# Expert routing: high and low part of the activations side by side in one 512-column product

## The reference

```python
s1, i1 = lax.top_k(s[:, :, 0], 16); s2, i2 = lax.top_k(s[:, :, 1], 16)
cand_s = (s1[..., :, None] + s2[..., None, :]).reshape(T, 8, 256)
top_s, pos = lax.top_k(cand_s, 16)
gate = softmax(top_s)
hid = einsum('td,thkd->thk', x, u[idx])
y = einsum('thk,thkd->td', gelu(hid) * gate, v[idx])
```

## Time and profile before

| | us |
|---|---|
| median of 3 runs (lowest, highest) | 2159.97 (2158.83, 2162.43) |
| the profiled execution, its own time | 2154.51 |
| its span, first to last instruction | 2152.7 |
| Gelu of tile 0 to Gelu of tile 127 in `peer_hidden` (start to start) | 1370.2 to 1785.58 |
| TensorE busy in the span | 1963.3 (91%) |
| VectorE busy in the span | 1616.8 (75%) |
| ScalarE busy | 982.0 (46%) |
| GpSimd busy | 437.4 (20%) |
| mean granted clock of TensorE, of full speed | 0.955 |

### The profile page before, as it was taken

The page is one execution under the profiler, slowest core; times in us unless marked ns, Lnnn a source line. Parts: engine busy times, 40 slices in busy tenths (PEclk is TensorE's granted clock), DMA queues, the critical chain, the costliest instruction groups (busy, mean ns, idle before and its releaser), DMA issues. The chain is left out here.

```text
span 2152.7 us, 40884 instructions
## 1 busy us (share of the span) xinstructions
PE 1963.3 (91%) x16381; PEld 1775.2 (82%) x16381; DVE 1616.8 (75%) x2682; ACT 982.0 (46%) x1758; POOL 437.4 (20%) x238
## 2 busy tenths in 40 slices
PE   8967899989779998998788888999999999999997
PEld 4954899988579997878787878999999998888886
DVE  3757787857658996776566574599999997877786
ACT  2527434336554333324344544454455554445553
POOL 1000000000230001431000300478677770000000
PEclk9979999989889998997899989999999999999999
DMA  7771698825148792312200034466566666777775
GB/s 251 254 201 60 229 341 310 287 108 193 64 147 292 284 342 89 103 55 81 79 4 4 2 138 157 154 219 206 188 196 200 199 205 216 243 243 240 241 243 192
DMA packets 184769, 390.65 MB, mean 181 GB/s; under 512 B 14922, under 2 KB 130298, under 8 KB 173050
## 3 DMA queue, kind: packets, MB, share of 16 engines
q1 hardware_dynamic: 166050, 371.21, 51.5%
q10 hardware_dynamic: 18530, 16.82, 2.3%
HBM read 368.58 MB, written 19.40 MB: 180 GB/s over the span
## 5 line engine op out<-in xcount | busy, mean ns | idle before, releaser
L3443 POOL TENSOR_TENSOR peer_lo<-peer_u,peer_hi 128x1024 fp32r<-128x1024 f32 x117 | 299.1, 2561 | 108.4 <-ACT peer_hi L3573 108.3
L3620 PE MATMUL route_pa<-all_h_hi,peer_hi 128*128 128x256 f32 x1024 | 291.6, 285 | 8.3 <-POOL peer_lo L3443 6.5
L3621 PE MATMUL route_pa<-all_h_lo,peer_hi 128*128 128x256 f32 x1024 | 290.7, 284 | 0.0
L3622 PE MATMUL route_pa<-all_h_hi,peer_lo 128*128 128x256 f32 x1024 | 290.5, 284 | 0.0
L1466 ACT CAST peer_hi<-peer_u 128x1024 fp32r<-128x1024 f32 x126 | 132.8, 1054 | 174.4 <-PE experts_py L1449 170.2
L3620 PEld LDWEIGHTS route_pa<-all_h_hi,peer_hi 128*128 128x128 f32 x1024 | 197.3, 193 | 9.9 <-POOL peer_lo L3443 7.9
L1445 PE MATMUL experts_py<-peer_hi,experts_c_hi 128*128 128x512 f32 x512 | 200.3, 391 | 3.6 <-DVE experts_c_lo L1506 3.6
L1446 PE MATMUL experts_py<-peer_lo,experts_c_hi 128*128 128x512 f32 x512 | 200.2, 391 | 0.0
L3621 PEld LDWEIGHTS route_pa<-all_h_lo,peer_hi 128*128 128x128 f32 x1024 | 197.3, 193 | 0.0
L3622 PEld LDWEIGHTS route_pa<-all_h_hi,peer_lo 128*128 128x128 f32 x1024 | 197.2, 193 | 0.0
L1728 PE MATMUL ffn_pa<-all_h_hi,ffn_u_hi 128*128 128x256 f32 x672 | 191.2, 285 | 3.0 <-DVE ffn_u_lo L1809 3.0
(11 more groups left out here) (608 smaller groups left out, 5313.8 us busy)
## 6 DMA issues: line engine op xcount, KB each, us to landing
peer_u<-in_peer_v SPq DMA_DIRECT2D x128, 512.0 KB, 3.8
peer_u<-in_peer_u SPq DMA_DIRECT2D x125, 512.0 KB, 3.6
l_w<-in_ffn_columns SPq DMA_DIRECT2D x44, 1024.0 KB, 8.8
ffn_ada_w<-in_ada_w SPq DMA_DIRECT2D x40, 1024.0 KB, 6.1
ffnw_v<-in_ffn_rows SPq DMA_DIRECT2D x44, 512.0 KB, 4.8
hid_kept<-peer_g ACTq DMA_DIRECT2D x128, 128.0 KB, 1.7
all_main<-hid_kept SPq DMA_DIRECT2D x128, 128.0 KB, 3.7
l_w<-in_diff_w_in SPq DMA_DIRECT2D x12, 1024.0 KB, 5.5
```

Of the source, the lines that this page charges most:

```text
L3443: pool.tensor_tensor(u_lo[:, i % ring, :], raw_u(i), u_hi[:, i % ring, :].bitcast(F32), ALU.subtract).then_inc(u_split, 1)
L3620: pe.matmul(out, u_hi[:, b, cols], h_hi[:, c, :], start=(c == 0), stop=False)
L3621: pe.matmul(out, u_hi[:, b, cols], h_lo[:, c, :], start=False, stop=False)
L3622: last = pe.matmul(out, u_lo[:, b, cols], h_hi[:, c, :], start=False, stop=(c == KT - 1))
```

## The change

From tile 49 on, for each of the 8 chunks, one matmul of 512 columns takes the place of two of 256: `u_hi` is multiplied with `h_hi` and `h_lo` side by side (`h_pair`), into the whole bank. The `u_lo` x `h_hi` matmul stays, and adds into the bank's first half. So the bank ends with two halves that must be summed: ScalarE copies the second half to `hid` (`keep_second`), VectorE adds the first half to it (`sum_rows`), and ScalarE takes Gelu in place in `hid` (`gate_summed`). TensorE may write the bank again when the sum two tiles before is made (`rows_summed`). ScalarE's order for tile i becomes: round tile i+2, copy the second half of tile i, Gelu of tile i-1, send tile i-1, the two copies of the quad. VectorE's loop goes by tiles: the one-hots of the quad after this tile's, the sum of the tile, the stores of this tile's quad. Tiles 0 to 48 are as before, and `h_hi`, `h_lo` become the two halves of `h_pair` for every stage.

```diff
@@ -3370,7 +3370,7 @@
     exp_at, turn_at, first_at = (27, 41), 47, 49
     quads_after = [[q for q in range(quads) if first_at + q * (tiles - first_at - 1) // quads == i] for i in range(tiles)]
     feed_v, feed_h = feeds
-    h_hi, h_lo = k["h_hi"], k["h_lo"]
+    h_hi, h_lo, h_pair = k["h_hi"], k["h_lo"], k["h_pair"]
     together = 4
     def raw_u(i):
@@ -3400,8 +3400,9 @@
         u_hi_ready, u_split, u_split_here, rows_ready, acted, shifted, exped, picked, turned, dve_done = (
             st.sem(n) for n in ("u_hi_ready", "u_split", "u_split_here", "rows_ready", "acted", "shifted", "exped", "picked", "turned",
                                 "dve_done"))
-        gate_ready, equal_ready, hot, product, copied, stored, v_split = (
-            st.sem(n) for n in ("gate_ready", "equal_ready", "hot", "product", "copied", "stored", "v_split"))
+        gate_ready, equal_ready, hot, product, copied, stored, v_split, second_kept, rows_summed = (
+            st.sem(n) for n in ("gate_ready", "equal_ready", "hot", "product", "copied", "stored", "v_split",
+                                "second_kept", "rows_summed"))
         block = st.block()
         def split(engine, i):
@@ -3499,6 +3500,11 @@
                     dve.wait_ge(copied, n + 1)
                     to = places(i, half)
                     dve.tensor_tensor(to, to, psum[:, n % banks, :, 0, :], ALU.add).then_inc(stored, 1)
+
+            def sum_rows(i):
+                dve.wait_ge(second_kept, i - first_at + 1)
+                to = hid[:, i % kept, :]
+                dve.tensor_tensor(to, pa[:, i % 2, 0:S], to, ALU.add).then_inc(rows_summed, 1)
             low_u(0)
             for t in range(TT):
@@ -3548,11 +3554,14 @@
             dve.tensor_copy(gates[:, 0, :], high.bitcast(F32)).then_inc(gate_ready, 1)
             dve.tensor_tensor(gates[:, 1, :], chosen[:, 2, :], high.bitcast(F32), ALU.subtract).then_inc(gate_ready, 1)
             dve.wait_ge(gate_ready, 3)
-            for i in range(quads):
-                one_hot(i)
-                if i >= 1:
-                    store(i - 1)
-            store(quads - 1)
+            one_hot(0)
+            for i in range(first_at, tiles):
+                for q in quads_after[i]:
+                    if q + 1 < quads:
+                        one_hot(q + 1)
+                sum_rows(i)
+                for q in quads_after[i]:
+                    store(q)
             for i in range(tiles, tiles + more):
                 dve.wait_ge(u_hi_ready, PIECES + i)
                 dve.tensor_tensor(u_lo[:, i % ring, :], raw_u(i), u_hi[:, i % ring, :].bitcast(F32), ALU.subtract
@@ -3578,6 +3587,15 @@
                     act.wait_ge(hid_kept_done[i % kept], 16 * (i // kept))
                 act.activation(hid[:, i % kept, :], pa[:, i % 2, 0:S], ACT.Gelu).then_inc(acted, 1)
+            def keep_second(i):
+                act.wait_ge(rows_ready, i + 1)
+                act.wait_ge(hid_kept_done[i % kept], 16 * (i // kept))
+                act.copy(hid[:, i % kept, :], pa[:, i % 2, S:2 * S]).then_inc(second_kept, 1)
+
+            def gate_summed(i):
+                act.wait_ge(rows_summed, i - first_at + 1)
+                act.activation(hid[:, i % kept, :], hid[:, i % kept, :], ACT.Gelu).then_inc(acted, 1)
+
             def keep_tile(i):
                 act.wait_ge(acted, i + 1)
                 act.dma_start(hid_kept[i], hid[:, i % kept, :]).then_inc(hid_kept_done[i % kept], 16)
@@ -3597,11 +3615,18 @@
                     t = exp_at.index(i)
                     act.wait_ge(shifted, t + 1)
                     act.activation(pick[:, t, 2, :], pick[:, t, 2, :], ACT.Exp).then_inc(exped, 1)
-                if i >= 1:
+                if i < first_at:
+                    if i >= 1:
+                        keep_tile(i - 1)
+                    gate_tile(i)
+                else:
+                    keep_second(i)
+                    if i > first_at:
+                        gate_summed(i - 1)
                     keep_tile(i - 1)
-                gate_tile(i)
                 for q in quads_after[i]:
                     low_table(q)
+            gate_summed(tiles - 1)
             keep_tile(tiles - 1)
         @block.tensor
@@ -3610,15 +3635,21 @@
                 b = i % ring
                 if i:
                     split(pe, i)
-                if i >= 2:
+                if i >= first_at + 2:
+                    pe.wait_ge(rows_summed, i - first_at - 1)
+                elif i >= 2:
                     pe.wait_ge(acted, i - 1)
                 out = pa[:, i % 2, 0:S]
                 for c in range(KT):
                     if i == 0 and c % 2 == 0:
                         pe.wait_ge(u_split_here, c // 2 + 1)
                     cols = slice(c * P, (c + 1) * P)
-                    pe.matmul(out, u_hi[:, b, cols], h_hi[:, c, :], start=(c == 0), stop=False)
-                    pe.matmul(out, u_hi[:, b, cols], h_lo[:, c, :], start=False, stop=False)
+                    if i < first_at:
+                        pe.matmul(out, u_hi[:, b, cols], h_hi[:, c, :], start=(c == 0), stop=False)
+                        pe.matmul(out, u_hi[:, b, cols], h_lo[:, c, :], start=False, stop=False)
+                    else:
+                        pe.matmul(pa[:, i % 2, :], u_hi[:, b, cols], h_pair[:, c].rearrange("p a s -> p (a s)"),
+                                  start=(c == 0), stop=False)
                     last = pe.matmul(out, u_lo[:, b, cols], h_hi[:, c, :], start=False, stop=(c == KT - 1))
                 last.then_inc(rows_ready, 1)
@@ -3657,8 +3688,8 @@
     half = P * NKEYS
     with Stage(nc, "all") as pst:
         k = {name: pst.sb(name, [P, P]) for name in ("ident", "ones", "iota")}
-        h_hi, h_lo = (pst.sb(n, [P, KT, S], F32R) for n in ("h_hi", "h_lo"))
-        k["h_hi"], k["h_lo"] = h_hi, h_lo
+        k["h_pair"] = pst.sb("h_pair", [P, KT, 2, S], F32R)
+        k["h_hi"], k["h_lo"] = (k["h_pair"][:, :, i, :] for i in range(2))
         chosen = pst.sb("chosen", [P, 3, S])
         small = Carved(chosen[:].rearrange("p a s -> p (a s)"))
         k["gains"], k["cols"] = small.sb("gains", [P, 6, KT]), small.sb("cols", [P, 2, KT])
```

## The result

The changed kernel takes 2175.99 us (median of 6 runs, 2171.44 to 2177.73), the kernel before, on the same chips, 2161.15 (6 runs, 2156.37 to 2165.2). The ratio is 1.007, with a 95% interval of 1.0054 to 1.0087: slower, as forecast. The forecast was 2178. The medians differ by 14.8. The profiled execution took 2171.54 with a span of 2169.8, 17.1 more than the span of the one profiled before.

What follows compares the result with a forecast made beforehand. Bound: mutual exclusion of GpSimd's subtraction and VectorE's two one-hots. Periods 16.8, end 2.4 and late tile 0.8 sum to 20.0 us, 15.6 with the tie the other way; 18 was taken, from 2160 to 2178, range 2157 to 2190.

Steps and rivals of the forecast that it cites:

- right of way: GpSimd's subtraction and VectorE's one-hots `equal` and `first` exclude each other, filling 20.15 of 20.16 us per six-tile period.
- The loop: Sum, Gelu, transfer, copies, cast, subtraction, one-hots, then a sum again: 7.54 us for two tiles, 3.77 a tile.
- The hold of the transfer's issue: The transfer's issue holds up ScalarE's queue for 0.33 us; at nothing, the periods would be 8.6 us shorter in all.
- The period: Tiles 54 to 126: six tiles take 21.60 us against 20.16, five take 17.74 against 16.62; 16.8 us more.
- The near tie: Behind a period's first quad, `first` and subtraction come within 0.05 us; where `first` wins, a period is about 0.34 shorter.
- TensorE's gain: One 512-column matmul for two of 256 saves 0.013 us a chunk, 0.107 a tile, 8.4 us in 79 tiles.
- The end: The last sum stands before the two splits of `v`, so the stage ends 2.4 us later.
- a late last tile: Tile 127 itself comes 0.8 us late, added to the end's cost.
- The start: The first five quads may cost 1 us more, or nothing.
- TensorE as the bound: Rival: VectorE and GpSimd overlap better, 8.4 us come back less 2.4 at the end, 2154; chance 0.10.
- Packed: Rival: sums hide beside subtractions, periods stay 19.68 to 20.16 us, total 2156 to 2162; chance 0.14.
- Not catching up: Rival: tiles without a quad do not restore the lead, each tile from 50 on takes 3.77 us, 2195; chance 0.06.

Runs made afterwards that it cites:

- Kernel 4: The kernel before, with the one-hots' constant key row copied once to PSUM and four banks instead of five for the quads' products; ratio 0.9961 to the kernel before.
- kernel 3: The kernel before with the 512-column product alone from tile 49 on, no copy or sum, `u_hi` x `h_lo` left out; ratio 0.9989 to the kernel before.
- kernel 1: The changed kernel with ScalarE's transfer of tile i-1 moved behind the table's copies; ratio 1.0027 to the kernel before.
- kernel 2: The changed kernel with ScalarE's Gelu and transfer of tile i-1 moved last, behind copies and cast; ratio 1.0042 to the kernel before.

## Why the prediction was right

*What bounds the stretch* was read rightly, and it was the step that decided. Kernel 4 shows it from one side (no right of way, TensorE's pace to the hundredth), kernel 3 from the other (a faster TensorE brings 0.1 of its 0.36 us).

*The loop* was forecast at 7.54 us for two tiles and is 7.52 where the period's late tiles run in it. The hold of the transfer's issue, one of the two unknowns, is real: the copies start 0.37 behind the start of the issue, and taking it out of the way gives 8.4 us in the 13 periods (kernel 1), where the prediction had 8.6.

*The period* was forecast at 21.60 and 17.74 us, and is 21.21 to 21.44 and 17.43 to 17.61. The near tie went the way that is cheaper: at 1550.73 `first` and the subtraction start together, `first` runs its 0.68 us, and the subtraction lasts 2.96 instead of 2.40. The block comes one tile later, at 1554.17 (2.89 us). So three tiles a period run at TensorE's 3.30, not two. It went this way in all 13 periods. The forecast for them was 16.8 us, and 12.4 with the tie this way; 13.5 were measured.

*TensorE's gain was mis-sized.* A chunk went from 0.36 to 0.353 us, not to 0.347: a tile of 2.82 instead of 2.776, 4.7 us in 79 tiles and not 8.4. The 0.227 came from a stage in which only 512-column matmuls follow each other; between 256-column ones it is 0.23 to 0.24. The Trainium skill (TensorE: Matmul & The Clock Gate, Back-to-back issue gap) gives its N/2.4 GHz + 2.5 ns for a single matmul apart and not for a stream with a weight load for each, which the prediction left out; the 1.6 us reckoned by it lie under the measured 4.7. As TensorE was not the bound, its gain did not come back in the total. But a period's sum has TensorE's time in it, as 2.98 and 3.26: each is 0.04 short, which by our estimate is some 0.9 of the 1.1 us between 12.4 and 13.5.

*The end* was forecast at 2.4 us, with 0.8 for a late last tile. It is 2.2 without the 0.8: the last two tiles have no one-hots before them, so the last sums came on time (T(126) to T(127) is 2.81). *The start* cost 1.2 where 1 or nothing was said.

*The number* is in part luck. The 18 was a middle between the tie's two ends, 20.0 and 15.6, and no sum of its own; with the tie as it went, 0.8 too much for a late last tile stood against 1.2 at the start and 1.1 in the periods that were not counted. The profiles give 17.1, the medians 14.8.

*The signs.* `second` took 1208 ns in the mean, as before, no sum took over 0.43 us, and TensorE did not wait for `u_lo`. Two signs did not come: matmuls of 512 columns 0.227 apart, and a wait for `second` in most tiles; it is 21 waits for 64 quads, and 10.2 of the 13.5 us stand where TensorE waits for the sum.

*The rivals.* TensorE as the bound is excluded by kernel 3. Packed, with no change, would have needed the cast early; kernel 1 comes nearer to it by 0.65 us a period in the mean, and kernel 2 shows a second wait that the rival had not named. Not catching up did not happen: in each period three tiles run at full pace behind the tile without a quad.

## What to carry to other kernels

An engine that is busy for 100% in a profile may be waiting: compare the length of the same instruction in different places, and a 2.89 beside a 0.68 tells that something holds it. Where two engines exclude each other, moving one constant operand to the other memory can be worth more than the work that one wanted to save: here 0.4% without any other change, and with it the change under study turns from 0.7% slower into 0.56% faster than the kernel before, most of it the constant's own doing. And when a result is handed on through three engines in order, look for the way back: added work in idle time is free, the same work in a loop is not.

## What was not expected of the hardware

A Gelu that reads SBUF takes 0.42 us where one that reads PSUM takes 0.38, for the same 128x256. When a VectorE instruction has the right of way first, GpSimd's subtraction is recorded as longer (2.96 instead of 2.40), so the wait shows on whichever engine lost, as busy time in both cases. And a 512-column matmul among 256-column ones keeps the next start 0.23 to 0.24 us away, against 0.227 among its like; why was not tried.
